# One hybrid layer on one core: new rotations, query roots in the exponentials, another order of TensorE and ScalarE work

## The reference, cut to what matters

```python
def rotate(x, cos, sin):
    m = x.shape[-1] // 2
    x1, x2 = x[..., :m], x[..., m:]
    return jnp.concatenate([x1 * c - x2 * s, x2 * c + x1 * s], axis=-1)

# attention: each head of 64 is normalized, has a gain, and its first 16 elements are rotated
q = partial_rope(rms_unit(q.reshape(hs)) * gq, cos, sin)
k = partial_rope(rms_unit(k.reshape(hs)) * gk, cos, sin)
s_own = jnp.einsum('bhqd,bhkd->bhqk', qc, ok) * HEAD_DIM ** -0.5   # masked, then softmax
# retention: whole heads of 64 are rotated
q = rotate(q.reshape(hs), cos, sin); k = rotate(k.reshape(hs), cos, sin) * HEAD_DIM ** -0.5
# S5: st[t] = a * st[t-1] + bu[t], complex a = mag * exp(i * angle), 1024 states
y = einsum(st_r, c_re) - einsum(st_i, c_im) + u * d
y = gelu(y); y = y * sigmoid(y @ w_glu)
```

## Time and profile before

| | us |
|---|---|
| three timed runs, median (lowest to highest) | 963.18 (962.85 to 967.78) |
| the profiled execution: its own time | 963.13 |
| its span | 961.2 |
| TensorE busy in the span | 923.2 |
| VectorE busy | 705.9 |
| ScalarE busy | 535.5 |
| GpSimd busy | 428.9 |

### The profile page before, as it was taken

One profiled execution on the slowest core, in us unless ns is written; L12 is line 12 of the kernel. 1 busy time (PEld: TensorE's weight loads), 2 busy tenths in 40 slices (PEclk: granted clock), 3 DMA queues, 4 the chain that ended last, 5 costly groups with the idle time before them and its releaser, 6 DMA issues.

```text
span 961.2 us, 20076 instructions
## 1 busy us (share of the span) xinstructions
PE 923.2 (96%) x5920; PEld 833.8 (87%) x5920; DVE 705.9 (73%) x1552; ACT 535.5 (56%) x1059; POOL 428.9 (45%) x340
## 2 busy tenths in 40 slices
PE   7988688999999999999999999999999999999998
PEld 5766577999999999999999999888888888888886
DVE  8998641205999902788888887788888888888886
ACT  6645443555545555555555555656656556655553
POOL 4774306577888888777777777200000000000000
PEclk9999889999999999999999999999999999999999
DMA  9542204026666666655555555777677776767773
GB/s 334 179 175 88 88 1 179 19 100 196 221 229 229 227 224 212 208 191 195 196 189 199 193 205 193 233 242 247 231 244 237 246 244 234 242 236 248 240 241 130
DMA packets 67595, 191.45 MB, mean 199 GB/s; under 512 B 6512, under 2 KB 8432, under 8 KB 67568
## 3 DMA queue, kind: packets, MB, share of 16 engines
q1 hardware_dynamic: 67568, 191.11, 58.7%
HBM read 173.78 MB, written 17.30 MB: 199 GB/s over the span
## 4 chain that ended last, share of the span: by engine, by line
PE 70%; POOL 11%; issue 7%; ACT 2%; DVE 2%; POOLq 0%; DVEq 0%
PE ps L416 21%; PE ps L417 21%; PE ps L418 21%; POOL w_lo L1515 10%; PE ps L686 3%; DVE routing L757 1%; ACT routing L1280 1%; PE ps L401 1%; POOL w_lo L1502 0%; ACT w_hi L1225 0%; PE ps L587 0%; ACT h_hi L1231 0%; DVE ps L757 0%; PE ps L578 0%; DVE ps L927 0%
## 5 line engine op out<-in xcount | busy, mean ns | idle before, releaser
L1412 ACT ACTIVATE w_hi<-raw 128x512 fp32r<-128x512 f32 x512 | 308.4, 628 | 137.2 <-PE ps L418 136.4
L1515 POOL TENSOR_TENSOR w_lo<-raw,w_hi 128x512 fp32r<-128x512 f32 x256 | 327.1, 1299 | 81.1 <-ACT w_hi L1412 80.9
L416 PE MATMUL ps<-h_hi,w_hi 128*128 128x256 f32 x1088 | 308.6, 284 | 2.5 <-POOL w_lo L1515 1.1
L417 PE MATMUL ps<-h_lo,w_hi 128*128 128x256 f32 x1088 | 307.9, 283 | 0.0
L418 PE MATMUL ps<-h_hi,w_lo 128*128 128x256 f32 x1088 | 307.9, 283 | 0.0
L757 DVE TENSOR_TENSOR w_lo<-raw,w_hi 128x512 fp32r<-128x512 f32 x256 | 177.4, 693 | 57.0 <-ACT w_hi L1412 42.0
L416 PEld LDWEIGHTS ps<-h_hi,w_hi 128*128 128x128 f32 x1088 | 208.8, 192 | 3.3 <-POOL w_lo L1515 1.3
L417 PEld LDWEIGHTS ps<-h_lo,w_hi 128*128 128x128 f32 x1088 | 208.8, 192 | 0.0
L418 PEld LDWEIGHTS ps<-h_hi,w_lo 128*128 128x128 f32 x1088 | 208.8, 192 | 0.0
L416 PE MATMUL ps<-w_hi,hot_gate 128*128 128x512 f32 x512 | 199.2, 389 | 0.0
L417 PE MATMUL ps<-w_lo,hot_gate 128*128 128x512 f32 x512 | 199.2, 389 | 0.0
(11 more groups left out here) (196 smaller groups left out, 883.6 us busy)
## 6 DMA issues: line engine op xcount, KB each, us to landing
raw<-in_u_t SPq DMA_DIRECT2D x128, 512.0 KB, 3.4
raw<-in_v SPq DMA_DIRECT2D x128, 512.0 KB, 3.4
act_spill<-acts SPq DMA_DIRECT2D x62, 256.0 KB, 2.1
acts<-act_spill SPq DMA_DIRECT2D x62, 256.0 KB, 3.4
routing<-in_w_in SPq DMA_DIRECT2D x5, 2048.0 KB, 11.7
routing<-in_w_out SPq DMA_DIRECT2D x2, 2048.0 KB, 7.9
routing<-in_w_q SPq DMA_DIRECT2D x2, 2048.0 KB, 7.8
xs<-in_x SPq DMA_DIRECT2D x2, 512.0 KB, 4.4
```

The costliest lines, as they stand in the source:

```text
L416: pe.matmul(dst, s_hi, m_hi, start=first and i == 0, stop=False)
L417: pe.matmul(dst, s_hi, m_lo, start=False, stop=False)
L1412: A.activation(w_hi[:, 2 * (s % 2) + h, :], raw[:, s, h * HALF:(h + 1) * HALF], ACT.Copy)\
L1515: G.tensor_tensor(w_lo[:, slot, :], raw[:, s, h * HALF:(h + 1) * HALF], w_hi[:, slot, :].bitcast(F32), ALU.subtract).then_inc(lo_ready, 1)
```

## The change

- The rotation tables are doubled on the host: the cosine twice side by side, the sine once negated and once plain. `rotate` then does four instructions over both token groups: two multiplies into a scratch tile, one multiply in place by the cosine, one addition. The tables come in two DMAs of 64 and 256 elements a partition instead of one of 160.
- Queries are no longer multiplied by their reciprocal root: only their rotated 16 elements get the gain, the other 48 gains are multiplied into the keys' gain columns, and the reciprocal root becomes the `scale` operand of the exponentials, and a factor on the maxima. One `root(32)` serves queries and keys.
- `phase_turns` loses the magnitude operation, which ScalarE does (`ACT.Abs`); `phase_turns(1)` follows `states(0)` and works in banks 6 and 7.
- VectorE's order: states(0), second angles, query heads, states(1), key heads, states(2), late scores, retention rotation, first-half scores, states(3).
- TensorE's order: `drive` and the turns come after more slices; `drive(3)` after slice 35; the products with C before the retention outputs.
- ScalarE's order: `phases(1)` after slice 15; the exponentials start after slice 33; the output projection's fifth and sixth slice copies stand ahead of the last two evacuations.

```diff
@@ tensor
             by_slices(1, range(3, KC))
-            by_slices(2, range(0, 3))
+            by_slices(2, range(0, 6))
             pe.wait_ge(states_ready, 1)
+            pe.wait_ge(turn_ready, 2)
             drive(1)
-            by_slices(2, range(3, KC))
+            by_slices(2, range(6, KC))
+            by_slices(3, range(0, 3))
             turn_heads(0)
-            by_slices(3, range(0, 6))
+            by_slices(3, range(3, KC))
             pe.wait_ge(states_ready, 2)
             drive(2)
-            by_slices(3, range(6, KC))
-            by_slices(4, range(0, 2))
+            by_slices(4, range(0, 4))
             turn_heads(1)
-            by_slices(4, range(2, 4))
+            by_slices(4, range(4, 6))
             late_scores(0)
-            by_slices(4, range(4, 6))
+            by_slices(4, range(6, KC))
             late_scores(1)
-            by_slices(4, range(6, KC))
+            by_slices(5, range(0, 2))
...
-            by_slices(5, range(0, 3))
-
+            by_slices(5, range(2, 4))
+            pe.wait_ge(states_ready, 3)
+            drive(3)
             pe.wait_ge(ret_rot_ready, 1)
...
-            by_slices(5, range(3, KC))
-            pe.wait_ge(states_ready, 3)
-            drive(3)
+            by_slices(5, range(4, KC))
@@ vector
-                step(V.scalar_tensor_tensor(pair(zb[:, js]), pair(xr[:, js]), -ROUND, turns, ALU.add, ALU.subtract))
-                V.scalar_tensor_tensor(xr[:, js], zb[:, js], -1.0, zb[:, js], ALU.mult, ALU.max).then_inc(turn_ready, 1)
+                V.scalar_tensor_tensor(pair(zb[:, js]), pair(xr[:, js]), -ROUND, turns, ALU.add, ALU.subtract)\
+                    .then_inc(turn_ready, 1)
...
+            def rotate(x_, m, tables, scratch):
+
+                heads = x_.shape[2]
+                cos, sin = (tables[:, f].unsqueeze(2).to_broadcast([P, TT, heads, 2 * m]) for f in range(2))
+                turned = scratch.rearrange("p (t h d) -> p t h d", t=TT, h=heads)
+                did(tt(turned[:, :, :, 0:m], x_[:, :, :, m:2 * m], sin[:, :, :, 0:m], ALU.mult))
+                did(tt(turned[:, :, :, m:2 * m], x_[:, :, :, 0:m], sin[:, :, :, m:2 * m], ALU.mult))
+                settle()
+                step(tt(x_, x_, cos, ALU.mult))
+                return tt(x_, x_, turned, ALU.add)
...
             states(0)
+            dve.wait_ge(turn_ready, 1)
+            phase_turns(1, 6)
+            dve.wait_ge(turn_ready, S5_C)
+            dve.wait_ge(consts_in, 96)
...
+            head_sums(0)
+            q4, k4 = by_head(0), by_head(1)
+            step(tt(q4[:, :, :, 0:ROPE], q4[:, :, :, 0:ROPE], gain(0, 0, ROPE), ALU.mult))
+            rotate(q4[:, :, :, 0:ROPE], ROPE // 2, rope, rot_tmp[:, 1024:1280]).then_inc(rot_ready, 1)
...
+            states(1)
+            head_sums(1)
+            dve.wait_ge(qk_sums, 2)
+            qk_var = variance(sums, 0, 32, 1.0 / HD)
+            step(tt(k4, k4, gain(1, 0, HD), ALU.mult))
+            step(rstd_of(qk_var, 0, 32, qk_rstd))
+            step(tt(k4, k4, qk_rstd[:, 16:32].rearrange("p (t h) -> p t h", t=TT).unsqueeze(3).to_broadcast([P, TT, MH, HD]),
+                    ALU.mult))
+            rotate(k4[:, :, :, 0:ROPE], ROPE // 2, rope, rot_tmp[:, 1024:1280]).then_inc(rot_ready, 1)
...
-            states(1)
-            heads(1)
+            states(2)
+            late_scores(0)
+            late_scores(1)
@@ scalar
                 A.activation(pS[:, js], zb[:, js], ACT.Sin, scale=-2 * PI_LOW).then_inc(phase_ready, 1)
+                did(A.activation(xr[:, js], zb[:, js], ACT.Abs))
+                settle()
                 A.activation(pc[:, js], xr[:, js], ACT.Sin, bias=quarter, scale=-2 * PI_LOW).then_inc(phase_ready, 1)
...
-                    A.activation(a, a, ACT.Exp, bias=hmax[:, g:g + 1], accum_out=hsum[:, g:g + 1]).then_inc(exp_ready, 1)
+                    q_at_ = 8 * (g // 8) + 2 * (g % 4) + g % 8 // 4
+                    A.activation(a, a, ACT.Exp, bias=hmax[:, g:g + 1], scale=qk_rstd[:, q_at_:q_at_ + 1],
+                                 accum_out=hsum[:, g:g + 1]).then_inc(exp_ready, 1)
...
-            slices_high(range(29, 35))
+            slices_high(range(31, 34))
             late_exps(0)
+            slices_high(range(34, 35))
+            late_exps(1)
             projected(3)
-            late_exps(1)
             slices_high(range(35, 37))
...
-            transposed_high(V_GM, 1, MIX_ORDER)
-            slices_high(range(FRONT + 4, FRONT + 2 * KC))
+            transposed_high(V_GM, 1, MIX_ORDER[0:6])
+            slices_high(range(FRONT + 4, FRONT + 6))
+            transposed_high(V_GM, 1, MIX_ORDER[6:8], 6)
+            slices_high(range(FRONT + 6, FRONT + 2 * KC))
```

More of the change, by code:

```diff
@@ L87 @@
 C_N = P + S
[L89 to L93, removed]
+ROPE_N = 2 * TT * ROPE
+TURN_N = 2 * TT * HD
 def slice_place(m):
@@ L560, in _ @@
                 turn(4 + b, [att0[:, b, h, :] for h in range(4)])
+            pe.wait_ge(c_ready, 1)
+            pe.wait_ge(states_ready, 4)
+            for c in range(S5_C):
+                signs = ((c_s[:, 0], pc), (c_neg[:, 0], zb), (c_neg[:, 1], xr), (c_neg[:, 1], pS))
+                for n, (w, st) in enumerate(signs):
+                    for j in range(4):
+                        mm = pe.matmul(ps[32 * j:32 * j + 32, 6, c * S:(c + 1) * S], w[:, 4 * c + j, :], st[:, 4 * c + j],
+                                       start=(n == 0), stop=(n == len(signs) - 1))
+            mm.then_inc(y_psum, 1)
             pe.wait_ge(rp_ready, 1)
@@ L579, in _ @@
             mm.then_inc(o_psum, 1)
[L581 to L589, removed]
             pe.wait_ge(pT_ready, 6)
@@ L731, in _ @@
             values_turn(TURNS - 1, last=True)
[L733 to L743, removed]
         @block.vector
@@ L817, in _, with phase_turns @@
             dve.wait_ge(full_dve, 4)
-            def phase_turns(c):
+            def phase_turns(c, bank):
                 js = slice(4 * c, 4 * c + 4)
-                turns = ps[:, 2:4, :].rearrange("p b (j t) -> p b j t", j=2)
+                turns = ps[:, bank:bank + 2, :].rearrange("p b (j t) -> p b j t", j=2)
                 pair = lambda a: a.rearrange("p (b j) t -> p b j t", b=2)
@@ L864, in _ @@
             dve.wait_ge(bb_ready, 1)
[L866 to L873, removed]
-                settle()
-                for x1, x2, co, si, ta, tb in views:
-                    did(tt(x1, x1, co, ALU.mult))
-                    did(tt(x2, x2, co, ALU.mult))
-                settle()
[L879 to L883, removed]
-                return ins
@@ new lines, in by_head, with head_sums, gain @@
+            def by_head(a):
+                return qk[:, :, a * MW:(a + 1) * MW].rearrange("p t (h d) -> p t h d", d=HD)
+            def head_sums(a):
+                dve.wait_ge(qk_sq, a + 1)
+                V.tensor_reduce(sums[:, 16 * a:16 * a + 16].rearrange("p (t h) -> p t h", t=TT),
+                                mv.rearrange("p t (h d) -> p t h d", d=HD), AX.X, ALU.add).then_inc(qk_sums, 1)
+            def gain(a, first, n):
+                return cols(V_GQK + a * HD + first, n).unsqueeze(1).unsqueeze(1).to_broadcast([P, TT, MH, n])
@@ L967, in _ @@
-            late_scores(1)
             dve.wait_ge(s_psum, 3)
@@ L1225, in slices_high, with transposed_high @@
                     A.activation(w_hi[:, m % 4, :], w_ring[n % W_SLOTS][:, k, :], ACT.Copy).then_inc(hi_ready, 1)
-            def transposed_high(gain, n, order=range(KC)):
-                for i, k in enumerate(order):
+            def transposed_high(gain, n, order=range(KC), first=0):
+                for i, k in enumerate(order, first):
                     act.wait_ge(t_psum, 4 * n + i // 2 + 1)
@@ L1348, in _ @@
             A.activation(rkT, ps[:, 3, :].rearrange("p (h t) -> p h t", h=2), ACT.Copy).then_inc(retT_ready, 1)
+            slices_high(range(37, 38))
+            act.wait_ge(max_ready, 3)
+            exps([(att0[:, g // 4, g % 4, :], g) for g in range(4)])
+            slices_high(range(38, 39))
+            exps([(att0[:, g // 4, g % 4, :], g) for g in range(4, MH)])
             slices_high(range(39, 40))
```

83 lines of the change are left out of this document (34 added, 49 removed).

## The result

| | before | after |
|---|---|---|
| median of 8 runs (lowest to highest), us | 964.54 (962.80 to 967.78) | 957.59 (955.15 to 958.92) |
| profiled execution: its own time | 963.13 | 956.80 |
| its span | 961.2 | 955.0 |

The ratio after to before is 0.9915, 95% interval 0.989 to 0.994: 7 us faster, under 1%. The forecast was 949.0, 14.1 us faster, range 943.5 to 956. The direction was right and the size half as large as forecast; the time lies outside the range.

A forecast was written before the change was run, and what follows sets the result against it. The prediction took VectorE's chain through four state quarters and two head passes up to 116.7 us, then TensorE's queue, then one GpSimd wait, as the bound. Sum: 963.1 - 9.9 - 4.2 = 949.0 us, range 943.5 to 956.

The forecast's parts named there:

- (a): First angles: VectorE loses a 1.2 us operation, ScalarE's Abs (1.05 us) is hidden; state quarter 0 starts 0.9 us earlier.
- (b): Second angles after states(0): TensorE waits 6 us before slice 8, then about 3 us at half level, 1.5 us lost.
- (c): VectorE's chain from drive(1) through states(1) and key heads beside GpSimd: keys ready at 73.5 us, bounds 70.1 and 74.3.
- (d): Negation to drive(3): TensorE idle 81 to 84.6 us for late scores, exponentials 1.4 us dearer, slice 35 at 94.3.
- (e): Retention rotation in four operations, 3.8 us and about 1.6 of contention; states(3) from 97.2 to 106.4 us.
- (f): Slices 36 to 39 end at 107.0 us; tail at full level, gate product ends at 125.5; gain 9.9 us.
- rival C: Attention tail: gaps between slices 34 to 39, then short matmuls, drop the clock; 956 us, chance 15%.
- (g): Output projection: the 2.9 us wait and the half level after it go; 4.2 us gained.
- A: Angles on ScalarE: Abs needs another table set than Sin, loads cost together 3 us; 952 us, chance 5%.
- B: Key heads: fewer SBUF-SBUF operations meet GpSimd busy, keys ready 3 us earlier; 946 us, chance 17%.
- D: Clock down from the fresh waits at 84 us on, not regained before the gate product; slower, 972 us, chance 5%.
- E: The part before 142.9 us gives nothing, only the output projection's gain stays; 958.9 us, chance 6%.

The follow-up runs named there:

- e3: Changed kernel with idle matmuls in TensorE's three long waits (before slice 8, the second late scores, slice 35): 951.57 us, ratio to before 0.9864.
- e1: Changed kernel, but slice 8, first of the second projection, waits for the first angle set only: 949.42 us, ratio to before 0.9845.
- e2: Changed kernel with ScalarE's copies of slices 34 and 35 before the first late exponentials, fourth copy-out and slice 36 before the second: 951.66 us.
- e5: Changed kernel, but GpSimd subtracts only 8 of 512 columns for slices 24 to 30, a test and no usable version: 948.81 us.
- e11: The changed kernel again, unaltered, on another occasion: 957.16 us, ratio to before 0.9914.
- e6: Changed kernel with ScalarE's order in the output projection as it was before: 960.55 us, ratio to before 0.9943.
- e9: Changed kernel with idle matmuls only in the two late waits, before the second late scores and before slice 35: 955.72 us.
- e7: Changed kernel with rotations in twelve operations, from the doubled tables: 954.16 us, ratio to before 0.9893.
- e10: Changed kernel with rotations in twelve operations and idle matmuls in TensorE's three long waits: 952.93 us, ratio to before 0.9867.

## Why the prediction was wrong

By its own steps, from the profiled execution (us from the start; gate is the start of the gate product):

| | forecast | before | after |
|---|---|---|---|
| drive(1) starts | 50.9 | 41.5 | 51.5 |
| keys' turn starts | 73.5 | 74.7 | 74.9 |
| second late scores | 84.6 | 83.8 | 86.9 |
| slice 35 starts | 94.3 | | 98.4 |
| drive(3) starts | 95.7 | 103.4 | 101.3 |
| last of 40 slices ends | 107.0 | 103.4 | 114.6 |
| gate | 123.6 | 133.5 | 131.3 |
| gate to the end of the output projection | 32.2 | 36.4 | 32.2 |

The gate product starts 7.7 us late, and with it everything behind it: that is the whole of the 7.8 us by which the profiled time missed 949.0. 4.1 of them are there when slice 35 starts, 3.5 come between it and the last slice.

- **(a): right.** Abs costs 1.05 us and is hidden.
- **(b): right, its half level too short.** The wait before slice 8 is 6.15 us (forecast 6), and VectorE is idle before states(1). Behind the wait the half level lasts 5.3 us, not 3, and costs 2.6 us, not 1.5: from slice 8 to drive(1) it takes 11.0 us, in e3 8.4. The wait ended 0.5 us sooner than forecast, and states(1) starts 0.8 late. e1 shows what the wait as a whole costs, 8.2 us: it was seen in the unchanged line and priced, and it is larger than what e2 or e3 gave.
- **(c): 0.6 us more.** The root is out at 66.9, late by the 0.8 us from (b); rotation and multiply beside GpSimd then take 8.0 us to the keys (forecast 7.4). (The forecast's terms, four operations of 0.3 to 0.4 + 1.1, add up to its upper bound, 74.3, and not to the 73.5 that it took; measured is 74.9.) e5 shows the mechanism.
- **(d): the waits named, their surroundings priced too low.** TensorE's wait for `s_read`, ScalarE's for the maxima and the starved slices all came, and so did the price of a pointer scale, an exponential of 256 elements every 0.59 us instead of 0.49. Three terms were missing. The negation was taken at its row of 0.4 and cost 1.4, a one-input operation beside a busy GpSimd. The second tiny product took 1.19 us, not 0.16, with GpSimd at work beside it from 91.5. And the late scores ran at the half level after 4.10 us of waiting, though (b) had charged this for a wait of that kind; on the chain that is 0.5. With the 1.4 us from (b) and (c), and 0.2 of small change, slice 35 was 4.1 us late.
- **(e): right where it counts.** The retention rotation takes 3.8 us (forecast 5.4). States(3), forecast for 97.2, waits 3.85 us for drive(3), until 103.4, and is over at 112.6; the C products start at 118.8, so this cost nothing.
- **(f): the failed step, the full level from slice 35 to the last slice.** The prediction said itself that slices 34 to 39 come "with gaps of 0.8 to 2.6 us", took the full level for them, and put the fall of the clock into rival C with the tail as its place. It fell before the tail: slice 35, drive(3), the transposes and slice 36 took 9.3 us (98.4 to 107.7), where e11 takes 5.1 us for them at the full level; 1.1 of the difference comes back in a shorter wait behind them (0.55 us for 1.65, before slice 37). From slice 35 to the last slice's end it took 16.2 us against 12.7 forecast. e11 and e6 have this stretch at the full level, and there it takes 13.1 us: the level is 3.1 of the 3.5 us. e2 takes the wait before slice 35 away, and with it the level, and gains 5.9 us.
- **The level altogether.** It was under-charged in three places of one kind: 1.1 us in (b), 0.5 in (d), 3.1 in (f), 4.7 of the 7.7 us. Work beside a busy GpSimd is the other part, 0.6 in (c) and 2.0 in (d). e3 fills all three waits and gains 6.0 us, which holds the 1.5 us that (b) had charged.
- **(f) after the last slice: right.** 18.6 us from there to the gate product's end at clock 1.00 (forecast 18.5), no wait for states(3). Its sign for a wrong clock, under 0.9 in 107 to 125 us, looked behind the place where the clock was down, 98 to 107, so none of its three signs of being wrong came.
- **(g): right.** 36.45 - 32.17 = 4.3 us in the profiles (forecast 4.2); with the old order e6 is 4.2 us slower in the profiles and 3.0 in the medians.
- **Rivals.** C had the mechanism and the wrong place. A is excluded by the absent table loads; B went the other way; D did not come. E, nothing gained before 142.9, is nearest by its number, 958.9, and not far off in substance: of the 9.9 us forecast for that part 2.2 were left, and the two places that it names are those of e1 and e2. With C's mechanism known to apply after each wait near 3 us, the forecast should have charged it to the two waits that it had itself forecast at 3.6 and 2.6 us, 2 to 4 us, and the range should have reached 959.

What stays open: why executions of the same kernel regain the full level at different times. The price follows from it: up to the gate product the half levels cost 2.6 + 4.3 = 6.9 us in the changed kernel's one profile and 2.1 + 1.1 = 3.2 in its other, e11, each against e3. For the two late stretches e9 and e11 together give a range, 1.1 to 4.3 us, and no single price.

## What to carry to other kernels

Price a wait of the matmul engine (TensorE) with the half level behind it: in this kernel three waits of 3 to 6 us cost some 6 us more than their length, and whoever forecasts a wait has to charge this too, as a range, since it differs between executions. When work is moved, look for the waits that the move has made needless (the bank was no longer shared, the wait was still there, 8 us), and for in-order engines that wait for something late with early work queued behind (5.9 us). Beside a busy GpSimd count instructions of VectorE, not elements, but test whether they are on the path: four for twelve was worth about 1 us here.

## What the runs showed that was not expected

- A one-input scaling of 512 elements in SBUF takes 0.43 us with GpSimd still and 1.37 beside it; reductions of 1024 elements, also one-input, take 1.22 us in both cases.
- A longer VectorE rotation went with a shorter time (e7, 3.4 us by the medians, the ranges overlapping). By its profile the later keys cut TensorE's waiting into pieces, and from 88 us on the clock stayed up; with the clock held up in both, e10 is not faster than e3.
- Being later can be cheaper: in e11 TensorE reached slice 35 later, waited less, and kept its clock.
- It is not the length of one wait alone that goes with the fall. Behind 2.53 us in e5 and 2.34 in e7 the clock stayed at 1.00, behind 2.62 in e7 it fell, and behind the same 2.62 in e10 it stayed. In the profiles of e2, e3, e6 and e11 the output projection began at the half level, for some 3.4 us and at a price of 1.6, behind waits of 1.42, 1.04 and 0.77 us, which the other profiles have too, at the full level.
- Executions of the changed kernel spread over 4 us, 954.8 to 958.9; those of e5 over 0.5 and of e3, with the waits filled, over 0.5. The spread goes roughly with the mean granted clock, 0.991 in the three fastest and 0.987 to 0.989 in the others.
